# Ten RMS norms of a two-block fp32 kernel: token sums held per partition, high parts first, and other neighbours for three loads

## The reference, cut to what matters

```python
def rms_norm(x, g):
    y = xf * lax.rsqrt(jnp.mean(xf * xf, axis=-1, keepdims=True) + RMS_EPS)
    return (y * g)
...
x = x + 0.5 * swiglu(rms_norm(x, ffn1_norm), w1, w3, w2)      # na, then ffn1
h = rms_norm(x, mix_norm); p = h @ w_in                       # nb
...
x = x + (gate_a * y_a + gate_b * y_b) @ w_out
x = x + 0.5 * swiglu(rms_norm(x, ffn2_norm), ...)             # nc, then ffn2
x = rms_norm(x, final_norm)                                   # nd
x = x + 0.5 * g1x * swiglu_2(modulate(rmsnorm(x, norm_ffn1), sh1x, sc1x), ...)   # ne, then ffn3
ctx = ctx + 0.5 * g1c * swiglu_2(modulate(rmsnorm(ctx, ...)))                    # nf (context)
q, k, ... = project(modulate(rmsnorm(x / ctx, norm_mix), ...), w_in)             # ng (x), nh (ctx)
...                                                           # ni, then ffn4; nj at the end
```

## Time and profile before

| | |
|---|---|
| median of 3 runs | 1832.56 us (1832.21 to 1837.78) |
| profiled execution | 1838.37 us, its span 1836.6 us, mean clock 0.973 |
| PE busy | 97% of the span |
| DVE, ACT busy | 58%, 36% |
| DMA engines | mean busy under half, 146 GB/s |
| 256-column fp32r matmuls | 120 ns from start to start at full clock |

### The profile page before, as it was taken

One profiled execution on the slowest core, in us unless ns is written; L12 is line 12 of the kernel. 1 busy time (PEld: TensorE's weight loads), 2 busy tenths in 40 slices (PEclk: granted clock), 3 DMA queues, 4 the chain that ended last, 5 costly groups with the idle time before them and its releaser, 6 DMA issues.

```text
span 1836.6 us, 31577 instructions
## 1 busy us (share of the span) xinstructions
PE 1777.0 (97%) x13038; PEld 1600.9 (87%) x13038; DVE 1060.7 (58%) x1569; ACT 652.4 (36%) x763; POOL 5.2 (0%) x13
## 2 busy tenths in 40 slices
PE   6999999999999999999999999899999999999997
PEld 6999898666699899998888888788889889989997
DVE  6676747133366767666464554773156733767766
ACT  4333454011244433343212222332236524453332
POOL 0000000000000000000000000000000000000000
PEclk9999999579999999999999999999999999999999
DMA  6555556246524455533222232133223335544451
GB/s 237 190 180 177 209 192 241 69 162 230 214 80 167 166 188 180 180 138 115 91 91 99 84 114 91 69 138 115 92 82 114 100 110 184 184 154 177 176 189 59
DMA packets 37534, 267.69 MB, mean 146 GB/s; under 512 B 4192, under 2 KB 4448, under 8 KB 5456
## 3 DMA queue, kind: packets, MB, share of 16 engines
q1 hardware_dynamic: 36432, 262.37, 39.8%
q0 software_dynamic: 1024, 4.17, 0.6%
HBM read 265.48 MB, written 1.05 MB: 145 GB/s over the span
## 4 chain that ended last, share of the span: by engine, by line
PE 92%; DVE 4%; ACT 2%; issue 1%; DMA 1%; DVEq 0%; POOL 0%; SPq 0%; ACTq 0%
PE PS L329 24%; PE PS L330 23%; PE PS L331 23%; PE PS L542 2%; PE PS L543 2%; PE PS L544 2%; PE PS L562 2%; PE PS L976 2%; PE PS L671 1%; PE PS L407 1%; PE PS L1009 1%; PE PS L996 1%; ACT W_HI L316 1%; PE PS L673 1%; DVE NT L1443 1%
## 5 line engine op out<-in xcount | busy, mean ns | idle before, releaser
L329 PE MATMUL PS<-H_HI,W_HI 128*128 128x256 f32 (+1 forms) x2128 | 653.6, 307 | 21.0 <-DVE H_LO L1454 11.9
L330 PE MATMUL PS<-H_LO,W_HI 128*128 128x256 f32 (+1 forms) x2128 | 649.2, 305 | 0.0
L331 PE MATMUL PS<-H_HI,W_LO 128*128 128x256 f32 (+1 forms) x2128 | 648.8, 305 | 0.0
L316 ACT ACTIVATE W_HI<-RAW 128x2048 fp32r<-128x2048 f32 x213 | 407.2, 1912 | 589.0 <-PE PS L331 557.9
L324 DVE TENSOR_TENSOR W_LO<-RAW,W_HI 128x2048 fp32r<-128x2048 f32 x213 | 487.2, 2288 | 187.2 <-ACT W_HI L316 186.7
L329 PEld LDWEIGHTS PS<-H_HI,W_HI 128*128 128x128 f32 x2128 | 413.0, 194 | 41.2 <-issue 25.0
L330 PEld LDWEIGHTS PS<-H_LO,W_HI 128*128 128x128 f32 x2128 | 413.4, 194 | 15.3 <-issue 0.2
L331 PEld LDWEIGHTS PS<-H_HI,W_LO 128*128 128x128 f32 x2128 | 413.3, 194 | 15.1
L329 PE MATMUL PS<-HID_HI,W_HI 128*128 128x256 f32 (+1 forms) x704 | 218.4, 310 | 3.3 <-DVE XC L1504 3.3
L330 PE MATMUL PS<-HID_LO,W_HI 128*128 128x256 f32 (+1 forms) x704 | 217.9, 309 | 0.0
L331 PE MATMUL PS<-HID_HI,W_LO 128*128 128x256 f32 (+1 forms) x704 | 217.8, 309 | 0.0
(11 more groups left out here) (334 smaller groups left out, 1890.0 us busy)
## 6 DMA issues: line engine op xcount, KB each, us to landing
RAW<-stream SPq DMA_DIRECT2D x249, 1024.0 KB, 4.8
XC<-xin SPq DMA_DIRECT2D x2, 512.0 KB, 5.1
XC<-xin POOLq DMA_DIRECT2D x1, 1024.0 KB, 5.2
out<-NT POOLq DMA_DIRECT2D x2, 512.0 KB, 2.9
CON<-consts POOLq DMA_DIRECT2D x1, 548.0 KB, 6.0
LW<-lora POOLq DMA_DIRECT2D x1, 512.0 KB, 6.6
DFT<-dft POOLq DMA_DIRECT2D x1, 512.0 KB, 4.0
ROPE<-rope POOLq DMA_DIRECT2D x1, 256.0 KB, 3.5
```

Source lines behind the costliest of these rows:

```text
L316: nc.scalar.activation(W_HI[s % RING][:], RAW[u % RING][:], ACT.Copy).then_inc(hi_done, 1)
L329: nc.tensor.matmul(acc, w_hi, x_hi, start=first, stop=False)
L330: nc.tensor.matmul(acc, w_hi, x_lo, start=False, stop=False)
L331: return nc.tensor.matmul(acc, w_lo, x_hi, start=False, stop=last)
```

## The change

1. **Sums per token.** The squares become the stationary operand (128 features by 128 tokens), and a 128x2 matrix with one column of ones moves, so the sums land with tokens on partitions in a 128x2 corner of a bank. Root and reciprocal work on 128x2. Two matmuls (`norm_spread`) with the reciprocal, broadcast, as stationary and the identity moving bring it back as 128x256 in PSUM, from where DVE's scale reads it.
2. **High parts first.** All eight scales precede all eight subtractions; the first unit of the next phase runs its W_HI and W_LO by H_HI products for all tiles, waiting for H_HI alone, then the H_LO products. `three` has the same three products in another order.
3. **nd and ne joined.** One set of squares and a four-column moving matrix (ones, squared gains) gives both sums; the sums stand between the tiles of ffn2's last unit. ne's squares and sums are gone; the product of both reciprocals scales ne's rows first, nd's own result is written after.
4. **ffn3's last unit** takes the 8 main tiles first, then the 8 context tiles (256 columns each), with ng's sum after the tenth tile and its spread after the twelfth. It waits for both hidden tiles at its start.
5. **W_LO of the next phase's second unit** leaves the last down of each ffn; for nb, ne and ng it now follows the subtractions. nh's five `add_squares` come after it; nh's spread stands after the second unit of `ret_q`, and `rotate_q(0)` behind it on DVE. `ret_q` uses other banks.
6. In nb's gap TensorE runs `ada(4)`, the spread, `ada(8)`.

```diff
             def norm(name, tmp=NT):
                 for k in range(KT):
                     norm_sum(name, k, tmp)
...
-                last = nc.tensor.matmul(NORM_BANK[name], con("ones"), tmp[:, k], start=(k == 0), stop=(k == 7))
+                for tt in range(2):
+                    last = nc.tensor.matmul(sums(name), tmp[:, k, tt * P:(tt + 1) * P], SQW[:, k, 2 - 2 * tt:6 - 2 * tt] if w == 4 else
+                                            ONE3[:, 1 - tt:3 - tt], start=(k == 0 and tt == 0), stop=(k == 7 and tt == 1))
...
+            def norm_spread(name):
+                pe.wait_ge(S("norm_rec"), NORM[name] + 1)
+                for q in ((2, 3, 0, 1) if name == "nd" else (0, 1)):
+                    last = nc.tensor.matmul(spread_of(name)[:, q * P:(q + 1) * P], RSTD[:, q:q + 1].to_broadcast([P, P]), con("ident"),
+                                            start=True, stop=True)
+                last.then_inc(S("norm_spread"), 1)
...
+                    if t == 0:
+                        for k in range(KT):
+                            pe.wait_ge(S("norm_hi"), KT * NORM_H[h_name] + k + 1)
...
+                                two(tile(w), W_HI[sl][:, c:c + P], W_LO[sl][:, c:c + P], H_HI[:, 0, k], k == 0)
+                        for k in range(KT):
                             pe.wait_ge(S("norm_h"), KT * NORM_H[h_name] + k + 1)
...
+                            if i == 10 and then == "nd":
+                                for k in {4: (0, 1), 5: (2, 3), 6: (4,), 7: (5, 6, 7)}.get(m, ()):
+                                    norm_sum(then, k)
...
+                def down_last(s):
+                    wait_unit(s)
+                    pe.wait_ge(S("hid_lo"), f * FT + FT)
+                    for q in range(16):
+                        h, m = q // 8, q % 8
...
+                        if q == 9:
+                            norm(then)
+                        if q == 11:
+                            norm_spread(then)
...
-                    up_ctx(0)
-                    norm(h_name)
+                    up_ctx(0, (0,))
+                    norm_spread("nd")
+                    up_ctx(0, (1,))
                     up_ctx(1)
...
-            ada(12)
+            ada(4)
+            norm_spread("nb")
+            ada(8)
...
+                elif tile >= 6:
+                    pe.wait_ge(S("rq_out"), 4)
...
             def norm_rows(name, half, gain, shift=None, tmp=NT):
-                for k in range(KT + 2):
...
+                dve.wait_ge(S("norm_spread"), NORM[name] + 1)
+                for k in range(KT):
+                    scale(name, half, k, gain, tmp)
+                for k in range(KT):
+                    rest(name, half, k, shift, tmp)
...
-                split_lo(dve, s0 + 34)
-                add(10, range(8), m0 + 124)
+                if halves == 1:
+                    add(10, range(8), m0 + 124)
...
             norm("nb", 0, lambda k: par("nm", k))
+            split_lo(dve, PHASE["fox_qk"] + 1)
...
+            split_lo(dve, PHASE["ret_q"] + 1)
             for k in range(1, 6):
                 add_squares("nh", k, NT3)
+            reciprocal("nh")
             split_lo(dve, PHASE["ret_q"] + 2)
-            reciprocal("nh")
+            dve.wait_ge(S("norm_spread"), NORM["nh"] + 1)
```

More of the change, by code:

```diff
@@ L442, in up, with tile @@
                     sl = s % RING
-                    for w, k in ([(w, k) for k in range(KT) for w in range(2)] if t == 0 else
-                                 [(w, k) for w in range(2) for k in range(KT)]):
-                        if t == 0 and w == 0:
-                            pe.wait_ge(S("norm_h"), KT * NORM_H[h_name] + k + 1)
[L448 to L456, removed]
+                    def tile(w):
+                        return BK8[2 * t + w][:, 0:ROWS] if apart else BK8[2 * (t % 2) + w][:, 0:n]
@@ new lines, in up @@
+                    if t == 0:
+                        for k in range(KT):
+                            pe.wait_ge(S("norm_hi"), KT * NORM_H[h_name] + k + 1)
+                            for w in range(2):
+                                c = (w * KT + k) * P
+                                two(tile(w), W_HI[sl][:, c:c + P], W_LO[sl][:, c:c + P], H_HI[:, 0, k], k == 0)
+                        for k in range(KT):
+                            pe.wait_ge(S("norm_h"), KT * NORM_H[h_name] + k + 1)
+                            for w in range(2):
+                                c = (w * KT + k) * P
+                                last = nc.tensor.matmul(tile(w), W_HI[sl][:, c:c + P], H_LO[:, 0, k], start=False, stop=(k == KT - 1))
+                                if k == KT - 1:
+                                    last.then_inc(psum_ready, 1)
+                        return
@@ new lines, in up @@
+                    for w in range(2):
+                        for k in range(KT):
+                            c = (w * KT + k) * P
+                            if apart:
+                                last = three(tile(w), W_HI[sl][:, c:c + P], W_LO[sl][:, c:c + P],
+                                             H_HI[:, 0, k], H_LO[:, 0, k], k == 0, k == KT - 1)
+                            else:
+                                last = three(tile(w), W_HI[sl][:, c:c + P], W_LO[sl][:, c:c + P],
+                                             rh(k), rl(k), k == 0, k == KT - 1)
+                        last.then_inc(psum_ready, 1)
@@ L504, in cols @@
                     turns = s == s0 and first is not None
+                    sl = s % RING
+                    if turns and len(first) == 3:
+                        for k in range(kt):
+                            pe.wait_ge(S(first[0]), first[2] + k + 1)
+                            for w in range(tiles):
+                                c = (w * kt + k) * P
+                                two(BK8[banks[w]][:, 0:n], W_HI[sl][:, c:c + P], W_LO[sl][:, c:c + P], rhs_hi(k), k == 0)
+                        for k in range(kt):
+                            pe.wait_ge(S(first[1]), first[2] + k + 1)
+                            for w in range(tiles):
+                                c = (w * kt + k) * P
+                                last = nc.tensor.matmul(BK8[banks[w]][:, 0:n], W_HI[sl][:, c:c + P], rhs_lo(k), start=False, stop=(k == kt - 1))
+                                if k == kt - 1:
+                                    last.then_inc(psum_ready, 1)
+                        if behind is not None and 0 in behind:
+                            behind[0]()
+                        continue
                     for w, k in ([(w, k) for k in range(kt) for w in range(tiles)] if turns else
@@ L1311, in _ @@
             root("nd")
-            for k in range(KT):
-                square("ne", 0, k, "nd_x", k + 1)
-            root("ne")
+            act.wait_ge(S("ne_ssq"), 1)
+            A(STD[:, 2:4], STD[:, 2:4], ACT.Sqrt, scale=1.0 / DM, bias=par("epsr")).then_inc(S("ne_std"), 1)
             for k in range(KT):
@@ L1838, in _ @@
+            ctx_add(0)
+            ctx_add(1)
+            reciprocal("ng")
+            ctx_add(2)
+            ctx_add(3)
+            dve.wait_ge(S("norm_spread"), NORM["ng"] + 1)
+            for k in range(KT):
+                scale("ng", 0, k, lambda k: GAIN[:, 2, k:k + 1], NT)
+                if k % 2:
+                    ctx_add(4 + k // 2)
+            for k in range(KT):
+                rest("ng", 0, k, (24, 0))
+            split_lo(dve, PHASE["ret_q"] + 1)
             for k in range(1, 6):
```

133 lines of the change are left out of this document (99 added, 34 removed).

## The result

The changed kernel took 1856.93 us (median of 4 runs, 1856.33 to 1858.85), the kernel before, run beside it, 1835.08 (4 runs); the ratio is 1.0121, 95% interval 1.0099 to 1.0143. It is slower, as forecast, but by 21.9 us where 9.7 were forecast, and it lies above the forecast range of 1835 to 1849. Its profiled execution took 1856.33 us (span 1854.5) against 1838.37 (span 1836.6): 17.9 us between the two traces.

The account below looks back on a forecast made before the run. TensorE, busy 97% of the span, bounds the kernel. Gains of 9.8 us less 0.4, 13.5 and 5.6 give -9.7: the profiled 1838.37 becomes 1848.1, or 1842.3 against the median, 5.8 lower; range 1835 to 1849.

Parts of the forecast that it names:

- both losses: The two places forecast to lose time: nb, -13.5 us, and ng with nh, -5.6 us.
- nb: First loss: a2's load waits for the moved split, TensorE idles over 12 us, then half clock; -13.5 us.
- The chain: At each norm, start of STD to first scale: 1.3 us instead of 2.3, the whole chain 1.2 shorter.
- Record widths: Sums and spreads: each small matmul is two records of about 0.11 us, by the profile row, not the skill's rule.
- rival D: Two-column records take a few hundredths of a microsecond, five sums 1.0 us shorter each; 1837.3 us, chance 0.04.
- ng, nh: Second loss: squares behind the W_LO split, DVE waiting for nh's spread, half clock; -5.6 us (2.5 to 8).
- Rivals A and B: A: a2 isn't held at nb, 1827.3 us, chance 0.06. B: no loss at ng and nh, 1836.7, chance 0.12.
- I take +3.3: Gain at nc, chosen between +2.0 if the clock falls as before and +4.6 if it does not.
- I take +2.2: Gain at ni, chosen between +3.5 with full clock and +0.8 if longer at half than before.
- rival C: The clock falls at nc and ni as before or longer, and more at nb; 1847 us, chance 0.17.
- I count the sums to end at 813.2 as before: At nd: the sums within ffn2's last down end no later than before, so nd and ne gain +1.9 us.
- ends `ret_q`'s first unit at about 1188.3: Behind ng: TensorE finishes that unit 3.6 us sooner than the 1191.9 before.

Follow-up runs that it names:

- e3: The kernel before, with DVE's split of unit 34 (W_LO) alone moved behind nb's rows: 1849.28 us against 1837.4, ratio 1.0062.
- e8: e1 with DVE's wait for nh's spread moved behind rotate_q(0) and the split after it: 1839.58 us.
- e2: e1 with the splits of the second units of ffn3 and ret_q also put back ahead of the last adds: 1841.78 us.
- e4: The changed kernel plus unread 256-column matmuls at nc and ni, 4 between sum and spread, 9 behind the spread: 1849.9 us.
- e1: The changed kernel with DVE's split of unit 34 put back ahead of ffn1's last adds: 1842.21 us, ratio to before 1.0029.

## Why the prediction was wrong

**Right.** The direction and both losses. *nb*: a2 behind the moved split on SP, 11.75 us without work, and e3 makes the whole of it with one instruction. That -13.5 is met to the tenth is luck in part: against the kernel before, unit 33 began 12.4 us late (10.0 on the clock, and the trace had come 2.3 ahead) where 11.0 was summed, and the half clock behind it cost 1.2 where 2.5 was. *The chain*: 1.27 us where 1.3 was summed; the first matmul of nc at 614.55 against 614.3. *Record widths*: 0.11 us for a record of two columns, so rival D is out, and the row goes over the rule. The Trainium skill ("TensorE: Matmul & The Clock Gate", on the 56 ns of a warm matmul) says that nothing starts closer than about 25 ns. The trace agrees with that as a floor; taken as a price it is too low here by a factor of four. The price seems to follow the stationary operand, which each record loads anew (as many PEld records as PE records in the earlier trace rows): 0.11 us with 128 stationary columns, 0.06 with 64 though 128 columns moved. No run varied that alone. *ng, nh*: every link that the text lists; the wait for the spread cost 3.1 (e8), the split ahead of the squares 4.1 with the clock (e2). Rivals A and B did not come.

**Wrong: the size,** 17.9 where 9.7 was summed, and the range with it. Two steps failed: the price of the clock at five norms, and the reference from which the sum was taken.

*The clock.* "I take +3.3" at nc and "I take +2.2" at ni: the first matmul of nc was as forecast, but the mean between full and half clock was too kind. The unit had 6.8 us at half both times; measured +1.7 and +0.6, and with the clock held (e4) +4.3 and +3.3, near the +4.6 and +3.5 that the text gives for that case. This is rival C, which had 0.17: its +2.0 and +0.8 were right to 0.3, and fourteen falls in fourteen say that it was the likelier. Its own total, 1847, would still have missed by 10 us, since it too names no clock at nd.

At nd "I count the sums to end at 813.2 as before" had no clock in it; the last sum began at 825.6, which is 815.6 less the 10.0 us of delay, and the 24 context matmuls ran at half behind it: -1.8 in place of +1.9. In executions where the clock holds at nd, the forecast stands (+1.7), so this term was right in five traces of eight and wrong in the one measured.

At ng "ends `ret_q`'s first unit at about 1188.3" took in the still head but no fall of the clock behind it; the unit ended 1.1 us later. And behind nh's sum the fall was priced at 1.8 us; it was 6.8 us at half, 3.4 lost. In the account these four places make 1.6 + 3.7 + 2.9 + 1.6 = 9.8 us of excess; na and the stretch behind `ret_k` came out 1.8 better and two others 0.2 worse: 8.2 between the two sums. The text knew that two-column sums "do little in the array", and drew the consequence at nc and ni alone.

*The reference.* The sum was made against the profiled execution of 1838.37 and then lowered by 5.8, to the median of three runs. Beside the later experiments the kernel before has medians of 1837.4 (23 runs), 1837.09 (29) and 1838.11 (11): the profiled one was the ordinary one, and 1832.56 a low draw of three. Without the step the forecast would have been 1848.1. Of the 14.6 us between 1842.3 and 1856.9, 8.2 are the sum, 5.8 this, and 0.6 the distance of the profiled execution from the median.

**Still open.** The fills show at nc and ni that work in the gaps keeps the clock, and the one trace with narrow fills that width matters at nc. For nd, ng and nh the narrow sums as the cause are argued, not shown. Nor is it known why the clock falls at nd in some executions and not in others. The Trainium skill ("TensorE: Matmul & The Clock Gate", part 1 on the clock gate) says of a kernel's start that the number of slow matmuls varies from run to run; three falls in eight traces of the same code are of that kind, in the middle of a kernel, but tell no cause. Single runs of one kernel differ by up to 12 us (e1), and the time goes with the mean granted clock: the slowest two of e1's twelve have 0.965 and 0.964, the fastest 0.973. So no price under 3 us here rests on times; they rest on the traces, one for each kernel.

## What to carry to other kernels

Before moving a step that frees a buffer, ask what is issued behind it on the load queue, and how long the consumer can go without: 2.3 us of DVE work moved 13 us down cost 12 us by itself. A seam between phases can look busy and still run at half clock, as nd did here: read the granted clock of each seam, not the busy share, and try wide work, even useless work, in it. A wait belongs in front of the instruction that needs it, not in front of its group.

## What was not expected of the hardware

- The clock fell to half while TensorE had records nearly without a gap (nd: 3.21 of the 3.40 us before the fall, then 14.81 of 15 us at a mean clock of 0.66), among them 32 of four columns. With 13 unread matmuls of 256 columns instead of stops it held at 1.00 (nc, ni), and with narrow ones of the same duration it did not at nc (0.72).
- Useless matmuls made the kernel before faster: 56 of them, 3.0 us (0.9981, interval 0.9970 to 0.9992).
- The same code in the same place fell in three executions and held in five; one such fall costs 3.5 us at nd (+1.7 against -1.8).
